# Reordering small attention steps between the compression products of a decoder trunk so that steps of one TensorE tiling stand together

## What is computed

```python
def compress(k_raw, v_raw, pe_k, pe_v, wk1, wk2, wv1, wv2):
    ...
    def phi(rows, pe, w1, w2):
        blk = rows[:, idx] + pe[None, None, :, None, :]
        flat = jnp.moveaxis(blk, 3, 2).reshape(b, n_cmp, g, CMP_LEN * hd)
        return jax.nn.silu(flat @ w1) @ w2
    ...
def nsa_core(q, q_pos, kc, vc, c_end, ks_blk, vs_blk, ov):
    s = jnp.einsum('bqgrd,bngd->bqgrn', q, kc).astype(jnp.float32) * SCALE
    p_cmp, _ = masked_softmax(s, valid_c, -1)
    o_cmp = jnp.einsum('bqgrn,bngd->bqgrd', p_cmp.astype(vc.dtype), vc)
    imp = jnp.einsum('bqgrn,nm->bqgm', p_cmp, ov)
    ...
    _, sel = lax.top_k(imp, min(SLC_TOP, n_slc))
    ...
```

## Time and profile before

| | us |
|---|---|
| median of 3 runs | 930.7 (930.26 to 930.87) |
| span of the profiled execution | 928.4 |
| TensorE busy | 910.2 |
| VectorE busy | 647.7 |
| ScalarE busy | 453.6 |
| compression and first gates, layer 0 | 231 to 336 |
| the same, layer 1 | 686 to 790 |

### The profile page before, as it was taken

How to read it: one execution, slowest core, us unless ns; L and a number is a source line. 1 busy time by engine, 2 the same in 40 slices (tenths; PEclk the granted TensorE clock), 3 DMA queues, 4 the chain that set the end, 5 groups by cost and what they waited for, 6 DMA issues and landing times.

```text
span 928.4 us, 22050 instructions
## 1 busy us (share of the span) xinstructions
PE 910.2 (98%) x8244; PEld 850.5 (92%) x8244; DVE 647.7 (70%) x1443; ACT 453.6 (49%) x888; POOL 187.6 (20%) x321
## 2 busy tenths in 40 slices
PE   6999999999999999999999999999999999999997
PEld 6999899988888799999999998999888878999996
DVE  6999766677666467656769995666766565775564
ACT  6444665565543454334543447655554434443352
POOL 1200000236658400000000000003574771000000
PEclk9999999999999999999999999999999999999998
DMA  8762985636979973333675576666469799435421
GB/s 330 286 227 106 419 332 205 260 125 219 306 217 303 294 290 154 137 137 128 247 254 215 194 293 258 256 271 279 161 196 297 241 270 327 167 142 197 162 91 52
DMA packets 66346, 209.91 MB, mean 226 GB/s; under 512 B 12208, under 2 KB 49776, under 8 KB 56256
## 3 DMA queue, kind: packets, MB, share of 16 engines
q1 hardware_dynamic: 57200, 187.67, 55.3%
q0 software_dynamic: 8896, 20.81, 7.2%
q10 hardware_dynamic: 144, 0.01, 0.0%
HBM read 202.48 MB, written 41.36 MB: 263 GB/s over the span
## 4 chain that ended last, share of the span: by engine, by line
PE 92%; DVE 4%; ACT 2%; issue 2%; DMA 1%; DVEq 0%; SPq 0%; ACTq 0%
PE bank L1019 64%; PE bank L1272 9%; PE bank L1032 4%; PE bank L1192 2%; PE bank L1306 2%; PE bank L1162 1%; PE bank L1154 1%; DMA x<-in_x 1%; PE bank L1402 1%; PE bank L1205 1%; PE bank L1374 1%; ACT paged_r L1531 1%; PE bank L1097 0%; PE bank L1251 0%; PE bank L1384 0%
## 5 line engine op out<-in xcount | busy, mean ns | idle before, releaser
L1771 DVE TENSOR_TENSOR big_r<-big,paged_r 128x1024 fp32r<-128x1024 f32 (+1 forms) x160 | 194.8, 1222 | 74.1 <-ACT paged_r L1531 73.1
L1019 PE MATMUL bank<-xnT_high_r,paged_r 128*128 128x288 f32 x768 | 231.8, 302 | 0.0
L1019 PE MATMUL bank<-xnT_r,paged_r 128*128 128x288 f32 x704 | 207.6, 295 | 0.0
L1019 PE MATMUL bank<-xnT_high_r,big_r 128*128 128x288 f32 x704 | 207.0, 294 | 0.0
L1531 ACT ACTIVATE paged_r<-big 128x1024 fp32r<-128x1024 f32 (+1 forms) x160 | 166.7, 1049 | 4.3 <-DMA big<-in_w_feat 2.7
L1019 PE MATMUL bank<-short_r,big_r 128*128 128x288 f32 x568 | 167.5, 295 | 0.0
L1019 PEld LDWEIGHTS bank<-xnT_high_r,paged_r 128*128 128x128 f32 x768 | 144.0, 188 | 5.1 <-issue 2.7
L1019 PEld LDWEIGHTS bank<-xnT_high_r,big_r 128*128 128x128 f32 x704 | 132.5, 188 | 0.0
L1019 PEld LDWEIGHTS bank<-xnT_r,paged_r 128*128 128x128 f32 x704 | 132.3, 188 | 0.0
L1019 PE MATMUL bank<-short_r,paged_r 128*128 128x288 f32 x440 | 130.9, 298 | 1.2 <-DVE big_r L1771 1.0
L1019 PE MATMUL bank<-kvp_r,paged_r 128*128 128x288 f32 x440 | 130.4, 296 | 0.0
(11 more groups left out here) (348 smaller groups left out, 1827.7 us busy)
## 6 DMA issues: line engine op xcount, KB each, us to landing
big<-in_w_tok SPq DMA_DIRECT2D x13, 2048.0 KB, 8.9
big<-in_w_feat SPq DMA_DIRECT2D x12, 2048.0 KB, 8.4
big<-in_w_gate SPq DMA_DIRECT2D x10, 2048.0 KB, 8.4
out_kept_dil<-in_cache_dil SPq DMA_DIRECT2D x16, 1020.0 KB, 12.8
paged<-in_pool SPq DMA_DIRECT2D x218, 64.0 KB, 4.5
big<-in_w_up SPq DMA_DIRECT2D x12, 1024.0 KB, 8.8
paged<-in_pool POOLq DMA_DIRECT2D x166, 64.0 KB, 5.1
big<-in_kv_win SPq DMA_DIRECT2D x4, 2048.0 KB, 8.7
```

What stands on the lines that cost most here:

```text
L1019: last = mm(out, l, r, start=(c == 0 and i == 0), stop=(c == n - 1 and i == 2))
L1771: v.tensor_tensor(l_part[:, rest], full[:, rest], h_part[:, rest].bitcast(FP32), ALU.subtract)\
```

## The change

It reorders entries of the list in `steps`, and three groups of matmuls within `spv cnew`. No instruction is added or taken away.

- `spv 0 d4` and `spv 1 d4` move one piece later, next to `spv mix`; `sturn anew` moves one piece earlier, next to `sturn mix`.
- `sgateA 0` now comes ahead of `sscore 0 cmp`, which is followed at once by `sscore 1 d4`.
- `kc 1` and `sscore 1 win` stand together, `kc 1` one piece later; `sscore 1 cmp` and its softmax step come after `sscore 0 slc0` and `slc1`.
- After the last piece `sturn 0 slc1` comes ahead of `spv 0 cnew`. Between the first gates, `spv 0 slc0` and `slc1` follow `spv 1 win` directly, a gate earlier; `sturn 1 cnew` comes before `gate 0 0 1`; `sturn 1 slc0`, `slc1` and `sgateC 0` stand together ahead of `gate 0 0 2`; `spv 1 cnew`, `slc0` and `slc1` stand together ahead of `gate 0 0 3`.
- In `cnew` the two products with 32-row stationaries are neighbours.

```diff
--- before.py
+++ after.py
@@ -322,25 +322,26 @@
            [("cpv", 1), ("pv", units[-1]), ("gateC", 1)] + w1_split(1, 1) + \
            [("sscore", 0, "win"), ("sscore", 0, "new")] + piece() + \
            [("sturn", 0, "d4")] + piece() + \
-           [("spv", 0, "d4"), ("sturn", 0, "mix"), ("sexp", 0, "win")] + piece() + \
-           [("spv", 0, "mix"), ("sturn", 0, "anew"), ("kc", 0)] + \
-           piece(("spv", 0, "anew"), ("soA", 0)) + piece(("sscore", 0, "cmp"), ("sexp", 0, "cmp")) + \
-           [("sgateA", 0), ("sscore", 1, "d4")] + piece(("cmpt", 0), ("sscore", 1, "mix"), ("sturn", 0, "win")) + \
+           [("sturn", 0, "mix"), ("sturn", 0, "anew"), ("sexp", 0, "win")] + piece() + \
+           [("spv", 0, "d4"), ("spv", 0, "mix"), ("kc", 0)] + \
+           piece(("spv", 0, "anew"), ("soA", 0)) + \
+           piece(("sgateA", 0), ("sscore", 0, "cmp"), ("sscore", 1, "d4"), ("sexp", 0, "cmp")) + \
+           piece(("cmpt", 0), ("sscore", 1, "mix"), ("sturn", 0, "win")) + \
            [("sexp", 1, "A")] + piece() + \
            [("vc", 0), ("spv", 0, "win"), ("sturn", 1, "d4")] + piece() + \
-           [("spv", 1, "d4"), ("sturn", 1, "mix"), ("imp", 0)] + piece() + \
-           [("impsum", 0), ("spv", 1, "mix"), ("sturn", 1, "anew")] + \
-           piece(("spv", 1, "anew"), ("soA", 1)) + piece() + [("kc", 1)] + \
-           piece(("sgateA", 1), ("sscore", 1, "win")) + piece() + \
-           [("sscore", 1, "cmp"), ("sexp", 1, "cmp"), ("sscore", 0, "slc0"), ("sscore", 0, "slc1"), ("sexp", 0, "slc")] + piece()
+           [("sturn", 1, "mix"), ("sturn", 1, "anew"), ("imp", 0)] + piece() + \
+           [("impsum", 0), ("spv", 1, "d4"), ("spv", 1, "mix")] + \
+           piece(("spv", 1, "anew"), ("soA", 1)) + piece() + piece(("sgateA", 1)) + \
+           [("kc", 1), ("sscore", 1, "win")] + piece() + \
+           [("sscore", 0, "slc0"), ("sscore", 0, "slc1"), ("sscore", 1, "cmp"), ("sexp", 1, "cmp"), ("sexp", 0, "slc")] + piece()
     out += [("cmpt", 1), ("sturn", 0, "cnew"), ("sscore", 1, "new"), ("hpost", 1, 1, 1), ("htail", 1, 1, 1), ("sturn", 0, "slc0"), ("sexp", 1, "win"),
-            ("imp", 1), ("spv", 0, "cnew"), ("sturn", 0, "slc1"), ("vc", 1), ("impsum", 1)] + splits(("gate", 0, 0), 0) + \
+            ("imp", 1), ("sturn", 0, "slc1"), ("spv", 0, "cnew"), ("vc", 1), ("impsum", 1)] + splits(("gate", 0, 0), 0) + \
            [("sscore", 1, "slc0"), ("sscore", 1, "slc1")] + splits(("gate", 0, 0), 1) + [("sturn", 1, "win"), ("sexp", 1, "slc")] + \
-           [("gate", 0, 0, 0), ("spv", 1, "win")] + splits(("gate", 0, 0), 2) + \
-           [("gate", 0, 0, 1), ("spv", 0, "slc0"), ("spv", 0, "slc1"), ("sturn", 1, "cnew"), ("soC", 0)] + splits(("gate", 0, 0), 3) + \
-           [("sturn", 1, "slc0"), ("spv", 1, "cnew"), ("gate", 0, 0, 2), ("sturn", 1, "slc1"), ("sgateC", 0),
-            ("osplit", 0), ("spv", 1, "slc0")] + splits(("up", 0, 0), 0, 1) + \
-           [("gate", 0, 0, 3), ("spv", 1, "slc1")] + splits(("up", 0, 0), 2, 3) + splits(("gate", 0, 1), 0) + \
+           [("gate", 0, 0, 0), ("spv", 1, "win"), ("spv", 0, "slc0"), ("spv", 0, "slc1")] + splits(("gate", 0, 0), 2) + \
+           [("sturn", 1, "cnew"), ("soC", 0), ("gate", 0, 0, 1)] + splits(("gate", 0, 0), 3) + \
+           [("sturn", 1, "slc0"), ("sturn", 1, "slc1"), ("sgateC", 0), ("gate", 0, 0, 2), ("osplit", 0)] + splits(("up", 0, 0), 0, 1) + \
+           [("spv", 1, "cnew"), ("spv", 1, "slc0"), ("spv", 1, "slc1"), ("gate", 0, 0, 3)] + \
+           splits(("up", 0, 0), 2, 3) + splits(("gate", 0, 1), 0) + \
            [("up", 0, 0, 0)] + splits(("gate", 0, 1), 1) + [("up", 0, 0, 1), ("up", 0, 0, 2)] + \
            splits(("up", 0, 1), 0) + [("up", 0, 0, 3), ("osplit", 1)] + splits(("up", 0, 1), 1)
     items = [(fh, i) for fh in range(2) for i in range(3)]
@@ -1387,11 +1388,11 @@
                         pe.wait_ge(*PJ.is_used(("vc", hb)))
                         mm(out[:, P:2 * P], pt[0:NS, 0:P], v_new[:, VCOL["win"]:VCOL["win"] + P], start=False,
                            stop=True, skip_group_check=True)
+                        mm(out[:, 2 * P:3 * P], pt[0:NS, P:2 * P], v_new[:, VCOL["slc"]:VCOL["slc"] + P],
+                           start=False, stop=False, skip_group_check=True)
                         for b in range(RB):
-                            mm(out[32 * b:32 * (b + 1), 3 * P:4 * P], PTc[hb][0:NCS, 32 * b:32 * (b + 1)],
-                               vcs[hb][0:NCS, P * b:P * (b + 1)], start=False, stop=True, skip_group_check=True)
-                        last = mm(out[:, 2 * P:3 * P], pt[0:NS, P:2 * P], v_new[:, VCOL["slc"]:VCOL["slc"] + P],
-                                  start=False, stop=False, skip_group_check=True)
+                            last = mm(out[32 * b:32 * (b + 1), 3 * P:4 * P], PTc[hb][0:NCS, 32 * b:32 * (b + 1)],
+                                      vcs[hb][0:NCS, P * b:P * (b + 1)], start=False, stop=True, skip_group_check=True)
                     else:
                         z = int(what[-1])
                         for pg in PG:
```

## The result

The changed kernel takes 939.96 us (median of 6 runs, 938.93 to 943.24) against 930.89 for the kernel before, a ratio of 1.0097 (95% interval 1.0083 to 1.0111). The direction was forecast, the size was not: 933.4 with a range up to 935.2. The profiled execution has a span of 938.8 us, 10.4 above the 928.4 of before.

What follows compares the result with a forecast made beforehand. TensorE, busy 98% of the span, was taken as the bound. Terms gained 0.38 us a layer, 0.76 in both; less 3.5 for pages, 2.74 lost: 930.7 becomes 933.4 us, range 927.6 to 935.2.

Steps and rivals of the forecast that it cites:

- Part 3: Second half of the compression stage: `spv 1 d4` joins `spv mix`, `sturn anew` joins `sturn mix`; gain 0.22 us a layer.
- Part 8: Gate stage: `spv 0 slc0`, asked 3.55 us sooner, waits for pages 1.25 and 2.25 us, 3.5 together; bounds 1.5 and 5.5.
- 1 first half: Compression stage: `spv 0 d4` moves to `spv mix`, `sturn anew` to `sturn mix`; gain 0.39 us a layer.
- 2 `sgateA 0`, scorings: `sgateA 0` goes ahead of `sscore 0 cmp`, which joins `sscore 1 d4`; gain 0.17 us a layer.
- 4, 5 `kc 1` and what follows: Later `kc 1` gains 0.32 us, the later small softmax takes it back; loss 0.2 together, bounds gain 0.35, loss 0.6.
- 6 gate stage, joining: Four visits to the 128*32 tiling become two, `cnew` runs into `slc`, one switch saved inside `cnew`; gain 0.9 us a layer.
- 7 turn bank: Behind `gate 1`, `sgateC 0` waits for ScalarE's copy of `slc0`; idle 1.1 us a layer, bounds 0.8 and 1.3.
- `kc 1` lost its idle: Sign: `kc` row without its 0.79 us idle, instead about 0.5 us before the second of the last four pieces.
- The idle of 0.3 to 0.4 us before the transposes of `cnew`: Sign in half 0: TensorE idles 0.3 to 0.4 us there because the `slc` weights come later.
- the case: Forecast's own case: turn-bank and page waits both real, 931.6 to 934.5 us, chance 0.46.
- The rival in which the switches win: Neither page nor turn bank stops TensorE: 927.7 us, 926.5 if the softmax move costs nothing, up to 928.8; chance 0.18.
- the pages in time: Rival: last page at least 1 us sooner in each layer, wait 1.5 us or less in all; 929.9 to 931.4 us, chance 0.24.

Runs made afterwards that it cites:

- experiment with the old order: Changed kernel with `spv 1 d4` and `sturn 1 anew` back in their old places; 938.08 us, ratio 1.0087.
- early page read alone: Kernel before, where only `spv 0 slc0` and `slc1` move a gate earlier, behind `spv 1 win`; 935.39 us, ratio 1.0070.
- earlier issues: Changed kernel, all engines' steps kept; SyncE issues eight selected-value pages ahead of the gate weights' first half, their second half after the last page; 933.05 us, ratio 1.0029.
- splits later: Changed kernel with the first two quarters of `gate 0 1`'s weights rounded and split one up step later each; 936.45 us, ratio 1.0067.
- copies first: Changed kernel, ScalarE and VectorE taking the gate weights' fourth quarter behind the copies of `sturn 1 slc0` and `slc1`; 938.22 us, ratio 1.0090.
- all four waits away: Changed kernel, `spv 0 slc0`/`slc1` behind gate 1, `sgateC 0` behind gate 2, `spv 1 d4`/`sturn 1 anew` back, `gate 0 1` splits later; 927.56 us, ratio 0.9973.
- fastest kernel: The kernel with all four waits away, where `spv 1 win` also goes behind `gate 1`; 927.18 us, ratio 0.9971.

## Why the prediction was right and wrong

Two steps of the prediction were wrong in kind and one in size. Part 3 and the end of the gate stage counted TensorE's own time and put the waits for a projection bank at nothing; they measured 0.88 and 1.09 us in each layer. Part 8 had the page wait, but at 3.5 us for both layers, where it measured 5.9, with no term for the half clock that can follow, 1.6 us more. Layer 0, by its own steps (from starts in the two timelines; the gate stage's joining is what is left there without the waits), and layer 1 where it differs:

| step | forecast, us a layer | measured | |
|---|---|---|---|
| 1 first half | gain 0.39 | gain 0.41 | held |
| 2 `sgateA 0`, scorings | gain 0.17 | gain 0.30 | held, small |
| 3 second half | gain 0.22 | loss 0.66 | a wait missed: `imp 0` |
| 4, 5 `kc 1` and what follows | loss 0.2 | gain 0.04 | within its bounds |
| 6 gate stage, joining | gain 0.9 | gain 0.8 | held |
| 7 turn bank | loss 1.1 | loss 1.15 | held |
| 8 pages | loss 1.25 and 2.25 | loss 2.6 and 3.3 | mechanism right, size off |
| half clock after 8 | none | loss 1.6, layer 1 | missed |
| projection bank, `up 0 0 2` | none | loss 1.1 | missed |

The two losses for pages are the rows' idle and 0.24 us that the block before could have been overlapped. For both layers the lines differ from the forecast by 1.8 (step 3), 2.4 (pages), 1.6 (clock) and 2.2 us (up), 8.0 in all; the other lines give some 0.5 back. So the two stages lose 10.2 us where 2.7 were forecast. The span's 10.4 has besides the 0.46 of its late start and an end that is 0.2 shorter.

**What held.** The price of a change of tiling was read rightly from one block: the weight load of the next block stands idle for 0.20 us, and a second block of the same form does not pay that again. By the Trainium skill (TensorEngine Tiling (Array Packing), Key Properties) a change of tiling mode drains the engine; that idle and the 1.66 us of the joined block agree. Of the signs that were named, `kc 1` lost its idle, and the second of the last four pieces has one of 0.54 us instead. The idle of 0.3 to 0.4 us before the transposes of `cnew` did not come: they start at 306.84, 0.12 behind the last matmul, and take 0.14 us longer than before.

**Step 3 failed** because it counted TensorE's time only. `imp 0` needs a projection bank that `hpost` (L1974) empties 1.2 us after the piece's end (281.62 against 280.44), behind a copy on VectorE. `spv 1 d4`, 1.0 us long, was that wait's cover, and the move took it away. The prediction looks at no bank in this part. The experiment with the old order shows the idle gone.

**The gate stage failed at its end.** Nothing in the prediction looks past `gate 3`, and so not at the bank of `up 0 0 2`. It is the same sort of miss: `spv 1 slc1` had been standing between `gate 3` and the up products.

**Step 8** was sized from one execution. Its margins (1.7 and 0.7 us) were right, and so was the sooner request, within 0.3 us: `gate 0` came 0.34 us later and not 0.6, so TensorE asked 0.28 and 0.22 us sooner than worked out. The rest is SyncE's pace. Its last page was issued 1.1 us later in layer 0 (315.9 against 314.8), with the first of them at the same time, 0.8 us later in layer 1, and landed some 5.8 us after its issue, as before. SyncE's queue, layer 0, before and changed:

```profile
304.19 4.36 SPq L843 DMA_DIRECT2D paged<-in_pool  x8
309.21 5.94 SPq L843 DMA_DIRECT2D paged<-in_pool  x9
...
304.18 4.81 SPq L844 DMA_DIRECT2D paged<-in_pool  x8
309.65 6.59 SPq L844 DMA_DIRECT2D paged<-in_pool  x9
```

What sets that pace is not shown. With the early page read alone, where all steps up to `spv 1 win` are those of the kernel before, the 9 issues took 7.81 us. Over the five profiled kernels with the wait in place, the wait is 1.79 to 3.08 us. The prediction put only the middle into its sum, and its range is narrower than its own bounds: with 5.5 us for the pages, the upper bound of part 8, its sum gives 935.4, and it ends the case at 934.5. The 5.9 us measured lie above that bound. And no rival had the clock.

The rival in which the switches win came near once the waits were gone, in a kernel that moves steps back to do it: 2.65 us below the kernel before (927.56 against 930.21), where 1.9 to 4.2 were worked out. The kernel with the earlier issues has the pages in time, but not that rival's 929.9 to 931.4 us: it takes 933.05, because the two waits for a projection bank stay. Page waits, half clock included, make 7.5 of the 10.4 us in the profiled execution.

Not settled: what made the whole trace 0.46 us late before the changed stage even begins (233.70 in the one, 234.16 in the other), which is within what these executions differ by (-0.13 to 2.74 us); what paces SyncE's issues; and where the half clock fell in runs without a profile.

## What to carry to other kernels

A small step between two large ones may be another step's cover: before moving it, list for the step behind it every buffer that it needs, banks too, and who empties each, and price the move with that idle. Joining blocks of one tiling is worth about 0.27 us a visit here, so one new wait of a microsecond eats four of them. A read of freshly fetched data that moves ahead of a 3.4 us product needs its loads issued sooner by those 3.4 us less the margin that they had, here 1.7 and 0.7; move the issues with it, or leave it.

## What the runs showed of the hardware

The half clock after a wait is not certain at a given length of idle. Granted clock after the page wait, by idle:

| kernel, layer | idle, us | clock after | 64 matmuls, us |
|---|---|---|---|
| changed, 1 | 3.08 | 0.50 | 3.52 |
| splits later, 0 | 3.06 | 0.50 | 3.33 |
| early pages alone, 0 | 2.90 | 1.00 | 1.96 |
| copies first, 0 | 2.55 | 0.50 | 2.68 |
| changed, 0 | 2.35 | 1.00 | 1.96 |
| five others | 1.79 to 2.06 | 1.00 | 1.95 or 1.96 |

In the kernel with copies first, layer 0, it falls later and stays, over half of `gate 1` (granted clock after POOL's column):

```profile
322.00:323.00 1.00, 1.00 (x40) 1.00 (x36) 0.00 (x0) 0.00 (x0) 0.00 (x0) 0.82 0.79 269
323.00:324.00 1.00, 1.00 (x24) 0.80 (x16) 0.00 (x0) 0.00 (x0) 0.00 (x0) 0.50 1.00 410
324.00:325.00 1.00, 1.00 (x11) 0.76 (x5) 0.63 (x3) 0.17 (x1) 0.00 (x0) 0.50 0.97 385
325.00:326.00 1.00, 1.00 (x6) 1.00 (x5) 0.89 (x4) 0.20 (x1) 0.00 (x0) 0.50 1.05 426
326.00:327.00 1.00, 1.00 (x9) 1.00 (x9) 0.89 (x4) 0.00 (x0) 0.00 (x0) 0.98 1.01 410
```

In the three stages with it, the half clock cost 1.3 to 1.6 us beside the wait itself. It is not tied to a long wait alone. The half clock at 14 us in the kernel with all four waits away came behind an idle of 0.98 us, and the kernel before idles 1.0 us at the same place and keeps 1.00. All twelve profiled executions have it in their last 4 to 8 us.

So the spread of a kernel's runs does not tell whether it has such a wait. Two kernels with the wait spread by 4.3 and 5.5 us (938.93 to 943.24; 934.79 to 940.26) and the one with all four waits away by 1.8 (926.79 to 928.60); but the one with the copies first, which has the wait, spreads by 1.8 (937.60 to 939.36), and the fastest kernel, which has none, by 3.6 (926.34 to 929.94).
